# Where the squares of eight attention heads are added up: VectorE adds four tiles, TensorE sums one

## The chip, the cores and the metric

The kernel runs on one core of one Trainium2 chip. The core's engines each work through their own list of instructions in order and wait for one another on semaphores: TensorE (PE; its weight loads are PEld), VectorE (DVE), ScalarE (ACT), GpSimd (POOL) and SyncE (SP). The metric is the device time of one execution in microseconds, lower is better; a kernel's time is the median of its runs.

## The reference, cut to what matters

The program is a transformer block followed by a second, hybrid one, on 512 positions of width 1024. The change lies in the first block, between its attention and its output projection. Eight heads of windowed attention and four of differential attention give the 1024 columns of `mix`. The first 512 columns are normed together, each head of the other kind by itself:

```python
y_a = swa_sink_attention(...)                  # (B, 512, 8 * 64)
y_a = rms_norm(y_a, swa_out_g[layer])          # one mean of squares over all 512 columns
y_b = diff_attention(...)                      # 4 heads of 128 columns, each normed over its 128
mix = jnp.concatenate([y_a, y_b], axis=-1)
x = x + rms_norm(jnp.einsum("bse,ed->bsd", mix, w_out[layer]), attn_post_g[layer])

def rms_norm(x, g):
    xf = x.astype(jnp.float32)
    xf = xf * lax.rsqrt(jnp.mean(xf * xf, axis=-1, keepdims=True) + EPS)
    return (xf * g.astype(jnp.float32)).astype(x.dtype)
```

## The kernel before

Activations stand transposed: the 128 partitions hold columns of the model, the free dimension holds the 512 positions, so `MIX[:, c, :]` is a tile of 128 columns by 512 positions. Tiles 0 to 3 are the eight windowed heads, tiles 4 to 7 the four differential heads. A sum over columns is then a sum over partitions, and TensorE makes it: a product of a constant matrix (`O512`, filled with 1/512) with a tile of squares gives the mean in every partition. For tiles 0 to 3 four such products accumulate in one PSUM bank, `PX[:, 1, :]`. They are plain fp32, and each appears in the trace as two matmul records.

The attention stage is one loop over 32 units, `for w in range(32)`, written out by hand for every engine. Units 0 to 15 are four pairs of windowed heads by four blocks of queries, units 16 to 31 four differential heads by four blocks. The order on each engine is the order of the code; there is no scheduler. The steps that matter here, with their lines:

- TensorE, for each unit: the scores two units ahead (`diff_scores`, L475), the transposes of this unit's probabilities (`att_turn`, L491), every fourth unit the product with the values (`swa_pv` L504, `diff_pv` L528), then two pieces of an unrelated projection that fills the gaps (`fill_piece`, L424: six matmuls each, weights split in a high and a low part). Each weight panel of this filler has eight pieces; pieces 0 to 3 make one output tile and 4 to 7 the next in the same PSUM bank, so piece 4 waits until VectorE has copied the first tile away: `pe.wait_ge(once("fill1_out"), k + 1)`. For panel k = 4 that is the first filler piece of unit 18. After it stands, at the end of unit 18, `mix_sums(0)` (L517).
- VectorE, for each unit: on even units the copy of a filler tile (`fill1_out`, L1345 or L1348), the logits two units ahead (`att_logits`, L1317), the probabilities one unit ahead (`att_probs`, L1325 to L1334), and at units 5, 9, 13 and 17 the copy of a pair's output into `MIX` (`swa_out`, L1361). `mix_scale` (L1366) multiplies `MIX` by the factor that the mean gives.
- ScalarE, for each unit: the exponentials (`att_exp`, L862) and the copy of the transposes (`att_copy`, L876 and L878); at unit 17 the four squares (`mix_square(0)`, L891), which wait for the last `swa_out`; at unit 19 the factor (`factor("mix", ...)`, L809 to L813).
- ScalarE and GpSimd or VectorE split each weight panel (`hi`, L776; L317, L1195).

`link(ins)` on VectorE issues an instruction and waits for it before the next one.

Of the kernel before, what the change touches and what calls it, by code (L numbers as in the profile page):

```python
# [21 lines left out]
ALU = mybir.AluOpType  # L22
# [61 lines left out]
def build(nc, panels, xT, cols_in, lamv_in, wi_in, rgw_in, uk_in, uv_in, outT):  # L84
    spill = nc.dram_tensor("x2_spill", (P, DC, S), F32, kind="Internal").ap()
    with ExitStack() as ctx:
# [3 lines left out]
        def at(name, shape, kb, dt=F32):  # L90
            size = 4
            for n in shape[1:]:
                size *= n
            assert kb * KB + size <= 207.5 * KB, (name, kb, size)
            return nc.alloc_sbuf_tensor_at(name, shape, dt, offset=ARENA0 + int(kb * KB))

        def sem(name):
            return ctx.enter_context(nc.semaphore(name))
# [22 lines left out]
        MSQ = at("MSQ", [P, DC, S], 96)  # L121
# [55 lines left out]
        O512 = at("O512", [P, P], 203)  # L177
        O128 = at("O128", [P, P], 203.5)
# [5 lines left out]
        PX = ctx.enter_context(nc.psum_tensor("PX", [P, 4, S], F32))  # L184
# [53 lines left out]
        def once(name):  # L238

            if name not in named:  # L240
                named[name] = sem(name)
            return named[name]
# [80 lines left out]
        def _(pe):  # L323
# [107 lines left out]
            def out_pass(o, p, t, c, c0, xh_first=False):  # L431

                s = p % 2
                wh, wl = (w[:, s].rearrange("p a b -> p (a b)")[:, (c - c0) * S + t * P:(c - c0) * S + t * P + P] for w in (WH, WL))
                pe.matmul(o, wh, XH[:, c, :], start=(c == c0), stop=False)
                pe.matmul(o, wh, XL[:, c, :], start=False, stop=False)
                return pe.matmul(o, wl, XH[:, c, :], start=False, stop=(c == c0 + 3))
# [68 lines left out]
                mm.then_inc(once("swa_pv"), 1)  # L506

            def mix_sums(k):
                tiles = range(4) if k == 0 else [3 + k]
                if k == 0:  # L510
                    pe.wait_ge(consts, 9)
                    pe.wait_ge(once("v_copied"), 5)
                else:
                    pe.wait_ge(once("mix_r"), k)
                for c in tiles:
                    pe.wait_ge(once("mix_sq"), c + 1)
                    mm = pe.matmul(PX[:, 1, :], O512[:] if k == 0 else O128[:], MSQ[:, c, :], start=(c == tiles[0]),  # L517
                                   stop=(c == tiles[-1]))
                mm.then_inc(once("mix_sum"), 1)

            def diff_pv(h):
                pe.wait_ge(once("att_copied"), 16 + NB * h + NB)
# [35 lines left out]
            low_piece(14)  # L558
            low_piece(15)
            mix_sums(4)  # L560

            p = FIRST["out1"][0] + 2
            pe.wait_ge(w_lo, p + 1)
            pe.wait_ge(once("att_logits"), 64)
            for c in range(4, DC):
                pe.wait_ge(once("mix_split"), c + 1)
                for t in range(4):
                    mm = out_pass(PG[:, t, :], p, t, c, 4)
# [4 lines left out]
            for t in range(4):  # L573
# [8 lines left out]
                for c in range(4, DC):  # L582
                    mm = out_pass(o, p, t, c, 4)
                mm.then_inc(once("y1_tile") if t < 3 else panel_done, 1)
            for t in range(2):
                pe.wait_ge(sq, 4 + t)
                mm = pe.matmul(PX[:, 1, :], O1024[:], SQY[:, 6 + t, :], start=False, stop=(t == 1))
# [72 lines left out]
            for t in range(4):  # L660
# [3 lines left out]
                for m in range(2):  # L664
                    pe.matmul(PX[:, m, :], RGW[:, 0, 2 * t + m, :], XC[:, t % 2, m, :], start=True, stop=True)
                    mm = pe.matmul(PX[:, 2 + m, :], RGW[:, 1, 2 * t + m, :], XC[:, t % 2, m, :], start=True, stop=True)
# [493 lines left out]
        def _(dve):  # L1160
            step_ = Count(dve_step)

            def link(ins):

                step_(ins)
                dve.wait_ge(dve_step, step_.n)
# [136 lines left out]
            def att_logits(w):  # L1303
                qb, s = w % NB, w % 3
                dve.wait_ge(once("att_s"), w + 1)
                if w >= 3:
                    dve.wait_ge(once("att_turned"), w - 2)
                n = (qb + 1) * P if w >= 16 else P if qb == 0 else 256
                if w < 16:
                    j = w // NB  # L1310
                    dve.tensor_copy(PD[s][:, :, n:n + 1], NSK[:, 2 * j:2 * j + 2].rearrange("p (a b) -> p a b", b=1))
                for m in range(2):
                    if w < 16:
                        dist, first, slope = NDS[:, 256 - n:], NSK[:, 2 * j + m:2 * j + m + 1], SLOPES_1[PAIR_HEADS[j][m]]
                    else:
                        dist, first, slope = NECF[:, (3 - qb) * P:], 3e38, SLOPES_1[8 + w // NB - 4]
                    dve.tensor_tensor_reduce(out=PD[s][:, m, 0:n], in0=dist, in1=PG[:, 2 * (w % 2) + m, 0:n],  # L1317
                                             scale=-slope, scalar=first, op0=ALU.add, op1=ALU.min,
                                             accum_out=NM3[:, 2 * s + m:2 * s + m + 1]).then_inc(once("att_logits"), 1)

            def att_probs(w):
                qb, s = w % NB, w % 3
                den = DEN3[:, 2 * s:2 * s + 2]
                dve.wait_ge(once("att_exp"), w + 1)
                link(dve.reciprocal(den, den))  # L1325
                if w < 16:
                    n = P if qb == 0 else 256
                    for m in range(2):
                        ins = dve.tensor_scalar(PD[s][:, m, 0:n], PD[s][:, m, 0:n], den[:, m:m + 1], None, ALU.mult)
                else:  # L1330
                    n = (qb + 1) * P
                    link(dve.tensor_scalar(RTL, den[:, 1:2], LAM, None, ALU.mult))
                    link(dve.tensor_scalar(PD[s][:, 1, 0:n], PD[s][:, 1, 0:n], RTL, None, ALU.mult))
                    ins = dve.scalar_tensor_tensor(out=PD[s][:, 0, 0:n], in0=PD[s][:, 0, 0:n], scalar=den[:, 0:1],  # L1334
                                                   in1=PD[s][:, 1, 0:n], op0=ALU.mult, op1=ALU.subtract)
                ins.then_inc(once("att_probs"), 1)

            def fill1_out(k, m):
                tile = FILL_TILES[k][m]
                if m == 0:  # L1340
                    dve.wait_ge(once("fill1_half"), k + 1)
                else:
                    dve.wait_ge(panel_done, FIRST["fill1"][0] + k + 1)
                if 6 <= tile < 10:
                    ins = dve.scalar_tensor_tensor(out=PROJ[:, tile, :], in0=PX[:, 2, :], scalar=SCALE / SLOPES_1[2 + tile],  # L1345
                                                   in1=R[:], op0=ALU.mult, op1=ALU.mult)
                else:
                    ins = dve.tensor_tensor(PROJ[:, tile, :], PX[:, 2, :], R[:], ALU.mult)  # L1348
                ins.then_inc(evac if m else once("fill1_out"), 1)

            def low_out(t):
                if t % 4 == 3:
                    dve.wait_ge(panel_done, FIRST["out1"][0] + t // 4 + 1)
                else:
                    dve.wait_ge(once("low_tile"), t + 1 - t // 4)
                dve.tensor_copy(Y1[:, t, :] if t < 4 else PROJ[:, 10 + t, :], PX[:, 2, :])\
                    .then_inc(evac if t % 4 == 3 else once("low_out"), 1)

            def swa_out(j):
                dve.wait_ge(once("swa_pv"), j + 1)  # L1360
                dve.tensor_copy(MIX[:, j, :], PX[:, 3, :]).then_inc(once("swa_out"), 1)  # L1361

            def mix_scale(k):
                dve.wait_ge(once("mix_r"), k + 1)
                for c in range(4) if k == 0 else [3 + k]:
                    dve.scalar_tensor_tensor(out=MIX[:, c, :], in0=MIX[:, c, :],  # L1366
                                             scalar=col("swa_out", c) if k == 0 else SUBLN,
                                             in1=MR[:], op0=ALU.mult, op1=ALU.mult).then_inc(once("mix_y"), 1)
# [7 lines left out]
            def diff_out(h):  # L1376
                dve.wait_ge(once("diff_pv"), h + 1)
                dve.tensor_copy(MIX[:, 4 + h, :], PX[:, 3, :]).then_inc(once("diff_out"), 1)
# [5 lines left out]
            for w in range(32):  # L1384
                if 2 <= w <= 24 and w % 2 == 0:
                    fill1_out((w - 2) // 4, 0 if w % 4 == 2 else 1)
                if w >= 26:
                    low_out(w - 26)
                if w + 2 < 32:
                    att_logits(w + 2)  # L1390
                if w + 1 < 32:
                    att_probs(w + 1)
                if w % NB == 1 and w >= 5:
                    swa_out(w // NB - 1) if w <= 17 else diff_out(w // NB - 5)
                if w >= 20 and w % NB == 0:
                    mix_scale((w - 20) // NB)
                if w == 24:
                    mix_lo(0)
                if w >= 25 and w % NB == 1:
                    mix_lo((w - 21) // NB)  # L1400
# [276 lines left out]
            for qb in (1, 2, 3):  # L1677
                w = MD[:, OFF[qb]:OFF[qb] + (qb + 1) * P]
# [183 lines left out]
```

## Time and profile before

| | |
|---|---|
| median of 3 runs | 1415.3 us (1414.84 to 1415.87) |
| the profiled execution's own time | 1418.66 us |
| its span in the trace | 1416.4 us |
| PE busy in the span | 1338.6 us (95%) |
| DVE / ACT / POOL busy | 857.8 / 580.5 / 232.7 us (61% / 41% / 16%) |
| mean granted TensorE clock | 0.971 of 2.4 GHz |
| chain that ended last | PE 79%, DVE 14%, ACT 3% |

The profile is of one execution. Its span runs from the first to the last recorded instruction; 2.3 us of the execution's time lie around it. Times in the rows are microseconds from the start of the span unless they are marked ns. TensorE's clock has two levels, 1.2 and 2.4 GHz; a granted clock of 1.00 is the upper one all through a stretch, and 0.50 the lower one.

### The profile page before, as it was taken

The page shows a single profiled execution, that of the slowest core. Times are in us where ns is not written, and L with a number is a line of the kernel's source. Part 1 is how long each engine was busy: PE and PEld are TensorE (multiplying, and loading weights), DVE is VectorE, ACT ScalarE, POOL GpSimd, SP SyncE. Part 2 cuts the span into 40 slices and gives each one's busy share as a digit, 9 for nine tenths or more (in the row PEclk, how much of TensorE's full clock was granted, in tenths as well). Part 3 has the DMA queues.
Part 4 walks back from the last instruction along what each step waited for, and adds up shares of the span by engine and source line. Part 5 has one row for each costly group of instructions (what it writes and reads, how often), then busy time and mean ns, then how long its engine had stood idle before and what let it go on. Part 6 is the DMA issues. An engine that isn't in the chain of part 4 may idle for free.

```text
span 1416.4 us, 16189 instructions
## 1 busy us (share of the span) xinstructions
PE 1338.6 (95%) x6006; PEld 1040.6 (73%) x6006; DVE 857.8 (61%) x1471; ACT 580.5 (41%) x848; POOL 232.7 (16%) x181
## 2 busy tenths in 40 slices
PE   7899979899999999999999999999799989999996
PEld 6676557688888888888888767777568855667885
DVE  6345664678888368738853333569987256663242
ACT  5344545444434233323322344323555246554231
POOL 2322113000000000000000323420004511114451
PEclk9999989899999999999999999899899999999999
DMA  5211002022232223222322221402113210001411
GB/s 188 89 60 60 31 30 89 30 89 89 93 113 91 89 91 115 91 89 92 115 89 89 90 115 65 149 32 87 60 64 115 90 60 30 31 30 63 162 73 60
DMA packets 17785, 116.48 MB, mean 82 GB/s; under 512 B 1984, under 2 KB 2240, under 8 KB 4544
## 3 DMA queue, kind: packets, MB, share of 16 engines
q1 hardware_dynamic: 16320, 108.35, 21.6%
q10 hardware_dynamic: 1408, 7.37, 1.4%
q8 instruction: 36, 0.59, 0.2%
q14 instruction: 21, 0.17, 0.0%
HBM read 111.52 MB, written 4.19 MB: 82 GB/s over the span
## 4 chain that ended last, share of the span: by engine, by line
PE 79%; DVE 14%; ACT 3%; issue 2%; DMA 0%; POOL 0%; ACTq 0%; DVEq 0%; SPq 0%
PE PG L337 20%; PE PG L338 20%; PE PG L339 20%; PE PX L424 4%; PE PX L689 3%; PE PX L598 2%; PE PG L718 2%; PE PX L728 1%; DVE MD L1565 1%; DVE XC L1591 1%; DVE MD L1583 1%; DVE WL L1195 1%; ACT WH L776 1%; PE PX L373 1%; DVE SM L1580 1%
## 5 line engine op out<-in xcount | busy, mean ns | idle before, releaser
L317 POOL TENSOR_TENSOR WL<-RAW,WH 128x512 fp32r<-128x512 f32 x168 | 229.4, 1397 | 1151.1 <-ACT WH L776 1151.1
L337 PE MATMUL PG<-XH,WH 128*128 128x512 f32 x992 | 392.7, 396 | 16.2 <-DVE WL L1195 9.3
L338 PE MATMUL PG<-XL,WH 128*128 128x512 f32 x992 | 388.3, 391 | 0.0
L339 PE MATMUL PG<-XH,WL 128*128 128x512 f32 x992 | 388.2, 391 | 0.0
L776 ACT ACTIVATE WH<-RAW 128x2048 fp32r<-128x2048 f32 x100 | 191.4, 1914 | 384.7 <-PE PG L339 374.5
L337 PEld LDWEIGHTS PG<-XH,WH 128*128 128x128 f32 x992 | 187.5, 189 | 62.9 <-DVE WL L1195 11.9
L338 PEld LDWEIGHTS PG<-XL,WH 128*128 128x128 f32 x992 | 187.6, 189 | 39.7 <-issue 1.4
L339 PEld LDWEIGHTS PG<-XH,WL 128*128 128x128 f32 x992 | 187.5, 189 | 39.4
L1195 DVE TENSOR_TENSOR WL<-RAW,WH 128x2048 fp32r<-128x2048 f32 x58 | 132.7, 2287 | 18.8 <-ACT WH L776 18.7
L337 PE MATMUL PG<-AH,WH 128*128 128x512 f32 x256 | 99.6, 389 | 0.0
L338 PE MATMUL PG<-AL,WH 128*128 128x512 f32 x256 | 99.6, 389 | 0.0
L339 PE MATMUL PG<-AH,WL 128*128 128x512 f32 x256 | 99.6, 389 | 0.0
L959 ACT ACTIVATE Z<-Z 128x512 f32<-128x512 f32 x32 | 20.3, 633 | 164.7 <-DVE Z L1489 164.7
L1473 DVE TENSOR_TENSOR U<-PG,R 128x1024 f32<-128x1024 f32 x32 | 39.2, 1224 | 53.2 <-PE PG L339 48.5
L339 PEld LDWEIGHTS PG<-AH,WL 128*128 128x128 f32 x256 | 48.1, 188 | 10.0
L337 PEld LDWEIGHTS PG<-AH,WH 128*128 128x128 f32 x256 | 48.1, 188 | 10.0
L338 PEld LDWEIGHTS PG<-AL,WH 128*128 128x128 f32 x256 | 48.1, 188 | 9.9
L1508 DVE TENSOR_TENSOR FA<-PG,FA 128x1024 f32 (+1 forms) x12 | 14.7, 1224 | 64.6 <-PE PG L339 64.6
L337 PE MATMUL PG<-RH,WH 128*128 128x512 f32 x128 | 49.8, 389 | 0.0
L339 PE MATMUL PG<-RH,WL 128*128 128x512 f32 x128 | 49.8, 389 | 0.0
L947 ACT ACTIVATE C<-U,COL 128x512 f32<-128x512 f32 x64 | 48.2, 800 | 0.1
L1484 DVE SCALAR_TENSOR_TENSOR C<-U,COL,C 128x510 f32<-128x510 f32 x64 | 45.1, 747 | 3.8
(291 smaller groups left out, 1980.2 us busy)
## 6 DMA issues: line engine op xcount, KB each, us to landing
RAW<-panels SPq DMA_DIRECT2D x100, 1024.0 KB, 4.7
x_spill<-XT ACTq DMA_DIRECT2D x1, 2048.0 KB, 6.3
XT<-x_spill ACTq DMA_DIRECT2D x1, 2048.0 KB, 7.8
outT<-SQ SPq DMA_DIRECT2D x4, 512.0 KB, 3.0
XT<-xT ACTq DMA_DIRECT2D x2, 512.0 KB, 6.3
XT<-xT SPq DMA_DIRECT2D x2, 512.0 KB, 8.9
RGW<-rgw ACTq DMA_DIRECT2D x1, 1024.0 KB, 4.8
UK<-uk ACTq DMA_DIRECT2D x1, 512.0 KB, 5.7
```

The lines of the kernel that those rows point to most:

```text
L317: ins = pool.tensor_tensor(WL[:, s].rearrange("p a b -> p (a b)")[:, piece], RAW[:, s, piece], WH[:, s].rearrange("p a b -> p (a b)")[:, p ...
L337: pe.matmul(o, WH[:, s, c, ms], xh[:, c, :], start=(c == 0), stop=False)
L338: pe.matmul(o, WH[:, s, c, ms], xl[:, c, :], start=False, stop=False)
L339: mm = pe.matmul(o, WL[:, s, c, ms], xh[:, c, :], start=False, stop=(c == DC - 1))
L424: mm = pe.matmul(PX[:, 2, :], w[:, s, c, m * P:(m + 1) * P], x[:, c, :], start=(c == 0 and w is WH and x is XH), stop=(c == DC - 1 and w i ...
L598: mm = pe.transpose(PX[:, m, kb * P:(kb + 1) * P], src[u % 3][:, m, kb * P:(kb + 1) * P], IDN[:])
L689: mm = pe.matmul(PX[:, 2, :], w[:, s, c, m * P:(m + 1) * P], x[:, c, :], start=(c == 0 and w is WH and x is XH), stop=(c == DC - 1 and w i ...
L776: act.activation(WH[:, s].rearrange("p a b -> p (a b)"), RAW[:, s, :], ACT.Copy).then_inc(w_hi, 1)
L947: ins = act.activation(C[:, b, m, :], U[:, b, m, :], ACT.Identity, bias=col("cb", k + 32 * m), scale=col("cw2", k + 32 * m))
L1195: dve.tensor_tensor(WL[:, s].rearrange("p a b -> p (a b)"), RAW[:, s, :], WH[:, s].rearrange("p a b -> p (a b)").bitcast(F32), ALU.subtrac ...
L1473: dve.tensor_tensor(U[:, b], psum_of(p0 + b), rr(), ALU.mult).then_inc(evac, 1)
L1484: step_(dve.scalar_tensor_tensor(out=C[:, b, m, 2:], in0=U[:, b, m, 0:S - 2], scalar=col("cw0", n + 32 * m), in1=C[:, b, m, 2:], op0=ALU.m ...
```

## The change

The squares are still ScalarE's. VectorE now adds tiles 2 and 3 onto tiles 0 and 1 in one instruction of 1024 elements, then tile 1 onto tile 0 in one of 512, right after the last `swa_out` at unit 17. TensorE waits for that sum (`mix_acc`) and makes one product where it made four. The sums of the four later heads stay as they were.

```diff
             def mix_sums(k):
-                tiles = range(4) if k == 0 else [3 + k]
                 if k == 0:
                     pe.wait_ge(consts, 9)
                     pe.wait_ge(once("v_copied"), 5)
+                    pe.wait_ge(once("mix_acc"), 1)
                 else:
                     pe.wait_ge(once("mix_r"), k)
-                for c in tiles:
-                    pe.wait_ge(once("mix_sq"), c + 1)
-                    mm = pe.matmul(PX[:, 1, :], O512[:] if k == 0 else O128[:], MSQ[:, c, :], start=(c == tiles[0]),
-                                   stop=(c == tiles[-1]))
-                mm.then_inc(once("mix_sum"), 1)
+                    pe.wait_ge(once("mix_sq"), 4 + k)
+                pe.matmul(PX[:, 1, :], O512[:] if k == 0 else O128[:], MSQ[:, 0 if k == 0 else 3 + k, :], start=True, stop=True)\
+                    .then_inc(once("mix_sum"), 1)
...
                 if w % NB == 1 and w >= 5:
                     swa_out(w // NB - 1) if w <= 17 else diff_out(w // NB - 5)
+                if w == 17:
+                    dve.wait_ge(once("mix_sq"), 4)
+                    link(dve.tensor_tensor(MSQ[:, 0:2, :], MSQ[:, 0:2, :], MSQ[:, 2:4, :], ALU.add))
+                    dve.tensor_tensor(MSQ[:, 0, :], MSQ[:, 0, :], MSQ[:, 1, :], ALU.add).then_inc(once("mix_acc"), 1)
                 if w >= 20 and w % NB == 0:
                     mix_scale((w - 20) // NB)
```

Two lines fewer stand ahead of them, so VectorE's steps have line numbers that are smaller by two in the kernel after. In the order of its instructions VectorE has, at the end of unit 17 and the start of unit 18, before (the copy L1361 is `swa_out`, L1345 is `fill1_out` for the tile that filler piece 36 waits for; the brackets name the semaphores that are waited for):

```order
L1334 SCALAR_TENSOR_TENSOR PD_62<-PD_62,SM 128x384 [waits dve_step]
L1361 COPY MIX<-PX 128x512 [waits swa_pv]
L1345 SCALAR_TENSOR_TENSOR PROJ<-PX,R 128x512 [waits fill1_half]
L1317 ISA PD_64,SM<-NECF,PG 128x128 [waits att_turned,att_s]
L1317 ISA SM 128x1
```

and after:

```order
L1332 SCALAR_TENSOR_TENSOR PD_62<-PD_62,SM 128x384 [waits dve_step]
L1359 COPY MIX<-PX 128x512 [waits swa_pv]
L1395 TENSOR_TENSOR MSQ<-MSQ 128x1024 [waits mix_sq]
L1396 TENSOR_TENSOR MSQ<-MSQ 128x512 [waits dve_step]
L1343 SCALAR_TENSOR_TENSOR PROJ<-PX,R 128x512 [waits fill1_half]
L1315 ISA PD_64,SM<-NECF,PG 128x128 [waits att_turned,att_s]
L1315 ISA SM 128x1
```

The two additions, with the wait for the four squares, stand ahead of the copy of the filler tile and of all that follows it on VectorE.

TensorE at the end of unit 18 and the start of unit 19, before (L424 is the filler, L475 the scores of unit 21, L491 the transposes of unit 19):

```order
L424 MATMUL PX<-XH,WL 128x512
L517 MATMUL PX<-MSQ,O_123 128x512 [waits mix_sq,v_copied,consts]
L517 MATMUL PX<-MSQ,O_123 128x512 [waits mix_sq] x3
L475 MATMUL PG<-PROJ 128x256 [waits att_logits]
L475 MATMUL PG<-PROJ 128x256
L491 MATMUL PX<-IDN,PD_63 128x128 [waits att_copied,att_probs]
```

and after:

```order
L424 MATMUL PX<-XH,WL 128x512
L516 MATMUL PX<-MSQ,O_123 128x512 [waits mix_acc,v_copied,consts]
L475 MATMUL PG<-PROJ 128x256 [waits att_logits]
L475 MATMUL PG<-PROJ 128x256
L491 MATMUL PX<-IDN,PD_63 128x128 [waits att_copied,att_probs]
```

Three products are gone, and nothing else changes its place on TensorE; the twelve filler matmuls of unit 18, the first of which waits for `fill1_out`, still stand ahead of the product.

## Rows read from the trace of the kernel before

**Rows 1.** The profile's page: engines' busy time; chain that ended last, by engine.

```profile
PE 1338.6 (95%) x6006; PEld 1040.6 (73%) x6006; DVE 857.8 (61%) x1471; ACT 580.5 (41%) x848; POOL 232.7 (16%) x181
...
PE 79%; DVE 14%; ACT 3%; issue 2%; DMA 0%; POOL 0%; ACTq 0%; DVEq 0%; SPq 0%
```

**Rows 2.** The chain in order of time, 137 to 147: start us, us, what.

```profile
137.60 0.68 DVE MIX L1361
138.28 0.61 DVE PROJ L1345
...
138.93 3.02 PE PX L424 x12
141.95 3.43 PE PX L517 x8
145.39 0.63 PE PG L475 x4
146.02 0.60 PE PX L491 x4
...
146.64 0.60 ACT PTD L878
```

**Rows 3.** Timelines of ACT, DVE, PE: start us, us, engine, line, operation, tiles [idle].

```profile
138.31 2.19 ACT L891 ACTIVATE MSQ<-MIX 128x512 f32<-128x512 f32 x4 [3.42 <-DVE MIX L1361]
...
138.20 0.68 DVE L1345 SCALAR_TENSOR_TENSOR PROJ<-PX,R 128x512 f32<-128x512 f32 x1
...
138.93 0.50 PE L424 MATMUL PX<-XH,WH 128*128 128x512 f32 x1 [0.65 <-DVE PROJ L1345]
```

**Rows 4.** DVE's groups by line and shape: additions of two SBUF tiles | busy, mean ns.

```profile
L1172 DVE TENSOR_TENSOR SQY<-SQY 128x1024 f32<-128x1024 f32 x5 | 6.1, 1223 | 0.8 <-ACT SQY L817 0.7
...
L1435 DVE TENSOR_TENSOR XT<-XT,Y 128x512 f32<-128x512 f32 x8 | 5.5, 683 | 0.0
```

**Rows 5.** PE's timeline: the first matmul after four waits for another engine.

```profile
55.63 0.69 PE L488 MATMUL PX<-IDN,PD 128*128 128x128 f32 x2 [3.64 <-DVE PD L1329]
...
162.74 0.50 PE L424 MATMUL PX<-XH,WH 128*128 128x512 f32 x1 [0.65 <-DVE PROJ L1345]
...
212.87 0.50 PE L435 MATMUL PX<-XH,WH 128*128 128x512 f32 x1 [2.49 <-DVE PROJ L1356]
...
250.11 2.05 PE L579 MATMUL PX<-SQY,O 128*128 128x512 f32 x2 [3.27 <-DVE SQY L1172]
```

**Rows 6.** Stretches: busy of PE, PEld, DVE, ACT, POOL, then PE's clock, DMA.

```profile
58.00:61.00 3.00, 3.00 (x9) 2.13 (x7) 0.00 (x0) 0.00 (x0) 0.00 (x0) 0.50 0.61 254
61.00:65.00 4.00, 4.00 (x21) 2.87 (x20) 1.66 (x8) 1.58 (x5) 0.00 (x0) 0.94 0.00 0
...
163.00:167.00 4.00, 4.00 (x12) 3.15 (x12) 1.71 (x6) 2.31 (x9) 0.00 (x0) 0.61 0.47 199
...
190.00:194.00 4.00, 4.00 (x10) 3.13 (x11) 1.61 (x6) 1.00 (x5) 0.00 (x0) 0.50 0.00 0
...
212.00:217.00 5.00, 3.87 (x14) 2.55 (x14) 2.98 (x6) 3.07 (x6) 3.64 (x3) 1.00 0.00 0
...
255.00:260.00 5.00, 4.41 (x14) 2.71 (x13) 0.69 (x1) 1.55 (x2) 0.00 (x0) 0.90 0.00 0
```

**Rows 7.** The chain in order of time: two later filler pieces at the low clock.

```profile
162.74 4.54 PE PX L424 x12
...
189.72 0.80 PE PX L435
...
195.00 0.86 PE PX L517 x2
```

**Rows 8.** POOL's timeline around the change, and the four scalings of tiles 0 to 3.

```profile
132.14 5.12 POOL L317 TENSOR_TENSOR WL<-RAW,WH 128x512 fp32r<-128x512 f32 x4 [14.89 <-ACT WH L776]
154.21 6.40 POOL L317 TENSOR_TENSOR WL<-RAW,WH 128x512 fp32r<-128x512 f32 x4 [16.95 <-ACT WH L776]
...
L1366 DVE SCALAR_TENSOR_TENSOR MIX<-MIX,COL,MR x4: 747/1260/1774, 153.4 to 156.5; 128x512 f32<-128x512 f32 x4
```

## The prediction, made before the change was run

> **What bounds the kernel now.** I read the page first: TensorE is busy for 95% of the span and carries 79% of the chain that ended last, VectorE 14% [rows 1]. That says only that TensorE's time is worth something on average, so the next view is the chain in order of time at the changed place. There it runs: VectorE copies the last pair's output (`swa_out`, 137.60), then the filler tile (`fill1_out`, 138.28), TensorE starts the filler at 138.93, runs twelve matmuls in 3.02 us, the four sums in 3.43 us, the scores and transposes of units 21 and 19, and hands over to ScalarE at 146.64 [rows 2]. Two things are to be seen. The four products do stand on the path, so what is taken from them is a gain. And the filler piece ahead of them is held up by VectorE: TensorE sat idle for 0.65 us until the filler tile was copied [rows 3]. There is no slack on VectorE at just the spot where the change puts new work. The timeline of ScalarE is the third view: the four squares start at 138.31, when the last copy into `MIX` is done, and take 2.19 us [rows 3].
>
> **What is removed.** Eight matmul records of the sums take 3.43 us on the path [rows 2], so a product (two records) is 0.86 us. The later single products agree: 0.86 us for two records at 195.00 [rows 7]. Three products go: 3 x 0.86 = 2.58 us less on the path, at the full clock.
>
> **What is added.** VectorE, done with `swa_out` at 138.28, now waits for the fourth square: 138.31 + 2.19 = 140.50, plus some 0.05 us to see the semaphore, 140.55. The addition of 1024 elements takes 1.22 us (five like it, both inputs in SBUF) and is waited for by the next one, which takes 0.68 us (eight like it) [rows 4]. With 0.04 us for that hand-over VectorE is free at 140.55 + 1.22 + 0.04 + 0.68 = 142.49. Instructions in a row overlap by some 0.08 us there (the filler copy started at 138.20, before the 138.28 at which the copy ahead ended) [rows 2, 3], so `fill1_out` starts at 142.41.
>
> **What is queued behind it.** The filler copy `fill1_out` was to start at 138.20 and now starts at 142.41: 4.21 us late. TensorE waits for it with the twelve filler matmuls of unit 18, and nothing else stands before them that it could do, since the scores of unit 20 and the transposes of unit 18 come earlier in its order. So the filler starts at 138.93 + 4.21 = 143.14, and TensorE's idle stretch grows from 0.65 to 4.86 us. The wait for `mix_acc` itself costs nothing: the sum is there at 142.49, and the product comes only after the filler, at 146.16. Behind `fill1_out` on VectorE stand the logits of unit 20 and the probabilities of unit 19, 0.5 and 1.7 us of work; 4.2 us late they are done before 146, and TensorE needs the latter at 147.7, after the product and the scores. ScalarE's exponentials lie between and are short. None of these becomes the path.
>
> Path at the full clock: +4.21 - 2.58 = +1.63 us when the scores of unit 21 begin. From there ScalarE's copy at 146.64 and all that follows [rows 2] hang on TensorE's transposes, and I find no wait behind them that ends by something unshifted: the chain has no DMA in it (0% [rows 1]), and the weight panels are fetched when a buffer comes free, so they move along. The shift reaches the end.
>
> **The clock.** This is the term that the timelines of before don't hold, since there TensorE waited for only 0.65 us at this place. After an idle 3.64 us at 55.63 the granted clock was 0.50 in 58 to 61 and 0.94 in 61 to 65, which makes it low until about 61.5: 5.9 us of the lower level, half of it lost, 2.9 us. After 3.27 us of idle at 250.11 it was 0.90 in 255 to 260, low until 256.0: 5.9 us again, 2.9 us lost [rows 5, 6]. Before 162.74 the idle time was 1.56 us and 0.65 us close together; the granted clock in 163 to 167 was 0.61 and the twelve filler matmuls took 4.54 us where those at 138.93 took 3.02: 1.52 us lost [rows 2, 5 to 7]. An idle 2.49 us before 212.87 left it at 1.00 [rows 5, 6]. The idle stretch here would be 4.86 us, longer than the first two, so I expect the lower level (1.2 GHz). The price has 0 at one end (it falls and rises again all within the wait, or not at all) and 2.9 us at the other. TensorE is on the path for 5.1 us at the full clock after the wait (3.02 + 0.86 + 0.63 + 0.60), so there is enough for either price to bite. I take 2.2 us, halfway between the 1.5 and the 2.9 that rows show. The Trainium skill, "TensorE: Matmul & The Clock Gate", section "What's actually happening", has it that "the default state is throttled, and activity releases the throttle". By that rule a pause in TensorE's work costs more than its length, and the sum is not +1.6 but about +3.8; the rows with the 3.64 and the 3.27 us of idle agree, the one with 2.49 us does not show it.
>
> **A rule against the additions.** The four scalings of `MIX` tiles, each 128x512 with two inputs in SBUF, took 747 to 1774 ns, and the slow ones lie in the 6.40 us from 154.21 in which GpSimd was splitting a panel [rows 8]. The additions are of the same kind. Between 137.26 (132.14 + 5.12) and 154.21 GpSimd does nothing [rows 8], and they run from 140.5 to 142.5, so I price them undisturbed. Were they to meet a panel, each could be longer by up to the 1.03 us between the fastest and the slowest scaling, 2 us in all. The Trainium skill, "SBUF — State Buffer", section "SBUF: two separate sides", says that a VectorE instruction with two SBUF inputs and a GpSimd one that reads SBUF take a shared port pair in turns, each for its whole length. By that rule alone the sum would be as much as 2 us worse; here the trace has the two apart.
>
> **Sum.** +4.21 - 2.58 + 2.2 = +3.8 us. Made against the profiled execution that is 1418.66 + 3.8 = 1422.5 us; that execution lies 3.4 us above the median of the runs, of which nothing belongs to the change. Against the median: 1415.3 + 3.8 = 1419.1 us.
>
> **Rivals.**
> - *No clock price.* The wait grows as worked out, but the clock stays up, or falls and rises within the wait. For it: 2.49 us at 212.87 cost nothing. Against it: 4.86 us is twice that, and both waits over 3 us are followed by the low level. Time: +1.6, 1416.9 us.
> - *Not slower: the later low stretches go.* A shift of the work changes where the later pauses fall, and with them whether the clock drops. At 162.74 the low clock cost 1.52 us, and from 189.72 to 195.00 twelve filler matmuls took 5.28 us instead of some 2.8 to 3.0, another 2.3 [rows 2, 7]. If both went, the sum would be 3.8 - 1.5 - 2.3 = 0.0, or -2.2 with no price at the new wait: 1413.1 to 1415.3 us. It decides as soon as the later pauses give back more than 3.8 us. Against it: these pauses are waits for VectorE that the change leaves in place, such as the 2.49 us at 212.87, and nothing shortens them.
> - *More than worked out.* The clock stays low on through unit 19 and into the pauses of the next units, as it is low all through 190 to 194 in the trace of before [rows 6]: 2 to 3 us more than my price, 1421.5 us.
> - *The change does less than it says*, that is TensorE gains little because the four products overlapped with something: against it, the eight records are back to back on the path. Its price would be at most the 2.58 us, giving 1421.7 us; I put it with the case before.
>
> **How the numbers follow.** A measurement of this kernel can tell 0.2%, 2.8 us, from no change; the bound for slower is 1418.1 us. The forecast (+2.4 to +5.2, as the clock price goes from 0.8 to 3.6) has 0.66, and nine tenths of that lie over the bound. No clock price has 0.20, all within 0.2%. Not slower has 0.07, of which some 0.04 is faster by over 0.2%. More than worked out has 0.07. Slower is 0.59 + 0.07 = 0.66, same 0.30, faster 0.04. The range takes in the case without a clock price with half a microsecond of room below and the one with a longer low stretch above: 1416.0 to 1421.5 us.
>
> **What would show it.** In the profile after: VectorE idle for about 2.2 us before the addition of 1024, until ScalarE's squares; additions of 1.22 and 0.68 us; TensorE idle for 4.9 us before the filler of unit 18, with VectorE's filler copy as the releaser; a single product of 0.86 us (1.7 at the low clock); a granted clock below 1.00 in the 4 us after the wait, and the twelve filler matmuls there over 4 us long; ScalarE's copy L876 (L878 before) 3.8 us later than at 146.64, and the same distance up to the end of the attention stage. The forecast is wrong if TensorE's idle stretch is much under 4 us (then something hid VectorE's wait), if the clock stays at 1.00 there, or if the distance at the end of the stage isn't that at unit 19 (then the later pauses decide).

## The result: 0.3% slower, as forecast

| | median, us | runs | range, us |
|---|---|---|---|
| before | 1415.76 | 7 | 1414.84 to 1416.42 |
| changed | 1420.49 | 7 | 1417.88 to 1421.93 |

The ratio is 1.0030, with a 95% interval of 1.0019 to 1.0041: +4.2 us, between +2.7 and +5.8. This ratio, like every ratio with an interval below, is estimated from all runs and is not the quotient of the two medians, which lie 4.7 us apart. The forecast was +3.8 us, 1419.1 us. The same kernel was measured again later beside 16 runs of the one before: 1.0018 (1.0009 to 1.0027), +2.6 us. Both intervals exclude no change, and both hold the forecast's ratio of 1.0027 or touch it.

### The profile page after: what moved, and what is told of

It is laid out like the page before. It is cut to its first block, busy times and chain, and to the rows that moved or that the text cites. A ratio compares the mean times of both kernels' runs of the same rounds, so it can differ in the third digit from the quotient of the medians.

```text
span 1418.6 us, 16179 instructions
## 1 busy us (share of the span) xinstructions
PE 1336.6 (94%) x6000; PEld 1039.9 (73%) x6000; DVE 859.7 (61%) x1473; ACT 580.6 (41%) x848; POOL 232.7 (16%) x181
## 4 chain that ended last, share of the span: by engine, by line
PE 79%; DVE 14%; ACT 4%; issue 2%; DMA 0%; POOL 0%; ACTq 0%; DVEq 0%; SPq 0%
PE PG L337 20%; PE PG L339 20%; PE PG L338 20%; PE PX L424 4%; PE PX L687 3%; PE PX L596 2%; PE PG L716 2%; PE PX L726 1%; DVE MD L1567 1%; DVE XC L1593 1%; DVE MD L1585 1%; DVE WL L1193 1%; ACT WH L774 1%; PE PX L373 1%; DVE SM L1582 1%
```

## The profile after

In the page of the changed kernel the engines' shares hardly move; TensorE is busy for 2.0 us less and the span is 2.2 us longer.

```profile
span 1418.6 us, 16179 instructions
...
PE 1336.6 (94%) x6000; PEld 1039.9 (73%) x6000; DVE 859.7 (61%) x1473; ACT 580.6 (41%) x848; POOL 232.7 (16%) x181
```

That is all a page can tell: an engine with less to do, in a longer execution. The chain in order of time (start us, us, what), at the place of [rows 2]:

```profile
136.90 0.61 DVE MIX L1359
137.51 0.02 issue
137.54 2.20 ACT MSQ L889 x4
139.73 0.02 issue
139.76 1.24 DVE MSQ L1395
141.00 0.02 issue
141.02 0.04 DVE MSQ L1396
141.06 0.57 issue
141.63 0.69 DVE PROJ L1343
142.32 0.04 issue
142.37 4.54 PE PX L424 x12
146.91 0.86 PE PX L516 x2
147.77 0.63 PE PG L475 x4
148.40 0.60 PE PX L491 x4
...
149.02 0.60 ACT PTD L876
```

Four squares on ScalarE and two additions on VectorE now stand on the path ahead of the filler tile's copy; before, the copy followed `swa_out` at once. (The chain splits the second addition's 0.69 us into 0.04 and 0.57 us of "issue", because the copy behind it waits for nothing but its turn on VectorE.) The product is down from 3.43 to 0.86 us, and the twelve filler matmuls between them are up from 3.02 to 4.54 us. VectorE's and TensorE's timelines name the waits (in brackets: idle before, and what ended it):

```profile
139.76 1.23 DVE L1395 TENSOR_TENSOR MSQ<-MSQ 128x1024 f32<-128x1024 f32 x1 [2.25 <-ACT MSQ L889]
141.02 0.69 DVE L1396 TENSOR_TENSOR MSQ<-MSQ 128x512 f32<-128x512 f32 x1
...
142.37 0.79 PE L424 MATMUL PX<-XH,WH 128*128 128x512 f32 x1 [4.86 <-DVE PROJ L1343]
```

The stretches show the clock (the number after POOL's):

```profile
137.00:142.00 5.00, 0.51 (x3) 0.27 (x3) 2.71 (x4) 3.97 (x9) 0.00 (x0) 0.68 0.59 210
142.00:146.00 4.00, 3.63 (x9) 2.90 (x10) 2.26 (x9) 0.88 (x4) 0.00 (x0) 0.55 0.00 0
146.00:150.00 4.00, 4.00 (x20) 2.52 (x20) 1.45 (x8) 0.96 (x2) 0.00 (x0) 1.00 0.00 0
```

It fell to the lower level inside the idle stretch, at about 138.8 (0.68 over five microseconds is 3.2 us at the lower level), and came back at 145.6 (0.55 over four microseconds is 3.6 us), 3.2 us after the filler had begun.

**A measure for this place.** Whole executions of one kernel differ by up to 6 us here (before: 1412.55 to 1418.71 us in 35 runs), so the experiments are judged by two numbers: the ratio over many runs, and a distance inside the trace, from the start of the squares on ScalarE to the start of its copy of unit 19. Before: 146.64 - 138.31 = 8.33 us [rows 2, 3]. Changed: 149.02 - 137.54 = 11.48 us, that is +3.15. This distance is free of what happened earlier in the execution and of later pauses. Counted from the start of the span the copy came only 2.38 us later (149.02 against 146.64), because this execution was already 0.77 us ahead when the squares began (137.54 against 138.31); that is why the page shows a span only 2.2 us longer.

## The experiments

### The additions moved behind the filler copy

```diff
-                if w == 17:
+                if w == 18:      # now behind fill1_out and att_logits(20), ahead of att_probs(19)
                     dve.wait_ge(once("mix_sq"), 4)
                     link(dve.tensor_tensor(MSQ[:, 0:2, :], MSQ[:, 0:2, :], MSQ[:, 2:4, :], ALU.add))
                     dve.tensor_tensor(MSQ[:, 0, :], MSQ[:, 0, :], MSQ[:, 1, :], ALU.add).then_inc(once("mix_acc"), 1)
```

> The changed kernel, with VectorE's wait for the squares and its two additions moved from the end of unit 17 to unit 18, behind the filler copy and the logits of unit 20. Theory (the loss is the filler copy queued behind the additions, plus the low clock that TensorE's 4.86 us of idle time bring): the filler starts 0.65 us after the transposes again, the additions run from about 0.9 us after the filler began and are done some 0.5 us after the filler ends, the probabilities of unit 19 are then what TensorE waits for; the path at ScalarE's copy of unit 19 is 1.7 us shorter than before, the clock stays at 1.00 there: 1.0 to 2.0 us faster than before, 1414 us. Rival A (the additions cost VectorE time wherever they stand, 1.9 us, because VectorE is the path): as slow as the changed kernel less the clock, +1.6 us. Rival B (the one product is no gain, since the four overlapped with something): no faster than before.

Measured: 1412.79 us against 1416.27, ratio 0.9975 (0.9967 to 0.9984). The instructions are those of the changed kernel, with VectorE's wait and its two additions behind the filler copy and the logits in place of ahead of them, and the result has the other sign. VectorE's and TensorE's timelines:

```profile
136.31 0.68 DVE L1343 SCALAR_TENSOR_TENSOR PROJ<-PX,R 128x512 f32<-128x512 f32 x1
...
138.64 1.23 DVE L1391 TENSOR_TENSOR MSQ<-MSQ 128x1024 f32<-128x1024 f32 x1 [1.25 <-ACT MSQ L889]
139.91 0.69 DVE L1392 TENSOR_TENSOR MSQ<-MSQ 128x512 f32<-128x512 f32 x1
...
137.04 0.50 PE L424 MATMUL PX<-XH,WH 128*128 128x512 f32 x1 [0.65 <-DVE PROJ L1343]
...
140.74 1.10 PE L516 MATMUL PX<-MSQ,O 128*128 128x512 f32 x2 [0.69 <-DVE MSQ L1392]
```

VectorE still waits for the squares (1.25 us), but while TensorE works on the filler. The filler starts 0.65 us idle, as before; the product now waits 0.69 us for the additions. The distance is 143.10 - 136.42 = 6.68 us, or -1.65, where the theory had -1.7. Two details of the expectation were off: the additions began 1.6 us after the filler and not 0.9, and what TensorE waited for was the additions, not the probabilities of unit 19. So rival A, by which the additions cost the same wherever they stand, is out, and so is rival B. The additions still cost 0.93 us of the 2.58 here, since the product waits for them, but no longer the 4.21 us that they cost ahead of the copy.

### The wait alone

```diff
                     swa_out(w // NB - 1) if w <= 17 else diff_out(w // NB - 5)
+                if w == 17:
+                    dve.wait_ge(once("mix_sq"), 4)
```

> The kernel before with one line added: at the end of unit 17 VectorE waits for the four squares, and adds nothing; TensorE still makes four products. Theory (the wait ahead of the filler copy is paid in full, and a long idle stretch of TensorE costs the clock on top): the filler copy starts 2.35 us later, TensorE is idle for 3.0 us in place of 0.65, the clock falls to the lower level for the filler: +2.35 + 1.5 = +3.9 us, at the least +2.35. Rival (the wait is hidden by slack on VectorE, the additions alone cost): 0 to +0.5 us.

Measured: 1419.64 us against 1416.27, ratio 1.0016 (1.0004 to 1.0027). One line that moves no data costs. The chain (start us, us, what):

```profile
138.52 2.20 ACT MSQ L891 x4
140.72 0.02 issue
140.74 0.70 DVE PROJ L1345
141.44 0.04 issue
141.49 5.49 PE PX L424 x12
146.97 3.54 PE PX L517 x8
150.51 0.63 PE PG L475 x4
151.14 0.60 PE PX L491 x4
...
151.76 0.60 ACT PTD L878
```

TensorE was idle for 3.00 us, the filler took 5.49 us against 3.02, and the distance is 151.76 - 138.52 = 13.24 us: +4.91. Of that 2.35 us is the wait, as expected, and 2.6 us the clock (2.47 in the filler, 0.11 in the products), 1.1 us more than I had set down. The clock was low from about 140.2 (0.78 in 138 to 142), before the filler began, until about 147.1:

```profile
142.00:147.00 5.00, 5.00 (x13) 3.86 (x12) 1.62 (x4) 1.26 (x7) 0.00 (x0) 0.50 0.00 0
147.00:152.00 5.00, 5.00 (x18) 2.42 (x18) 0.81 (x5) 0.23 (x1) 0.00 (x0) 0.99 0.00 0
```

The additions are not needed to explain a loss, and the rival's 0 to +0.5 us is out by the trace and by the ratio's interval (+0.6 to +3.8 us).

### One product and nothing else

```diff
-                tiles = range(4) if k == 0 else [3 + k]
+                tiles = [3] if k == 0 else [3 + k]
                 if k == 0:
                     pe.wait_ge(consts, 9)
                     pe.wait_ge(once("v_copied"), 5)
...
                 for c in tiles:
                     pe.wait_ge(once("mix_sq"), c + 1)
```

> The kernel before with TensorE's four products cut to the one of tile 3 alone and no additions, so the mean of squares leaves out tiles 0 to 2; it still waits for all four squares. Theory (three products of 0.86 us stand on the path): -2.6 us, with the clock as before at this place. Rival (the products overlap with other work): -0.5 us or less.

This kernel leaves three quarters of the columns out of the mean; it serves to time the path and nothing else.

Measured: 1412.84 us against 1416.27, ratio 0.9975 (0.9965 to 0.9985). The distance is 142.36 - 136.25 = 6.11 us, or -2.22, where 2.58 were taken out. TensorE's timeline says where most of the missing 0.36 us went:

```profile
139.72 1.02 PE L517 MATMUL PX<-MSQ,O 128*128 128x512 f32 x2
141.67 0.66 PE L491 MATMUL PX<-IDN,PD 128*128 128x128 f32 x4 [0.29 <-DVE PD L1334]
```

The transposes of unit 19 now wait 0.29 us for VectorE's probabilities, and those, by the chain, for ScalarE's exponentials, which are queued behind the four squares. With the products gone, what is late next is the squares themselves.

### TensorE kept busy in the wait

```diff
+                if w == 18:
+                    pe.wait_ge(once("v_copied"), 5)
+                    for _ in range(20):
+                        pe.matmul(PX[:, 1, 0:P], O1024[:], O1024[:], start=True, stop=True)
                 if w < 24:
                     fill_piece(2 * w)
```

> The changed kernel, with twenty 128x128 products of constants, whose result nobody reads, on TensorE ahead of the filler of unit 18, where it stood idle for 4.86 us. Theory (1.5 us or more of the loss is the clock that falls in that idle stretch): the filler starts at the same time after VectorE's copy, the granted clock stays at 1.00, the twelve filler matmuls take 2.8 to 3.0 us in place of 4.54, and the kernel is 1.5 to 3 us faster than the changed one, that is +1.6 us against before. Rival (the clock isn't what makes the filler slow, or the loss lies elsewhere): same time as the changed kernel, +4 us.

Measured: 1417.81 us against 1416.27, ratio 1.0004 (0.9993 to 1.0015). TensorE's timeline (two records for each of the twenty products), its chain, and the stretches with their clock:

```profile
137.05 4.63 PE L550 MATMUL PX<-O 128*128 128x128 f32 x40
142.07 0.50 PE L424 MATMUL PX<-XH,WH 128*128 128x512 f32 x1 [0.39 <-DVE PROJ L1347]
```

```profile
142.07 3.01 PE PX L424 x12
145.09 0.86 PE PX L516 x2
```

```profile
137.00:142.00 5.00, 4.68 (x42) 4.49 (x40) 2.71 (x5) 3.97 (x9) 0.00 (x0) 1.00 0.59 210
142.00:146.00 4.00, 3.93 (x16) 2.68 (x18) 1.96 (x9) 0.88 (x4) 0.00 (x0) 1.00 0.00 0
```

The filler starts as late as in the changed kernel, but the clock stays up and it takes 3.01 us. The distance is 147.20 - 137.24 = 9.96 us: +1.63, which is the sum at the full clock to the hundredth. The clock is thus shown to be a term of its own: 1.52 us in the first trace of the changed kernel. That rests on the trace: the interval of the ratio (-1.0 to +2.1 us) holds +1.63 and no change alike, and excludes only the rival's +4.

### The changed kernel again

> The changed kernel once more, unedited, with more runs. Theory (the change itself makes 1.6 us, the low clock behind the wait 1.5 to 2.6, as in two traces so far): +3.2 to +4.2 us against before, and in the trace a step of that size at the filler of unit 18, with less than 1 us more from there to the end of the attention stage. Rival (later pauses add to it in each execution): a further step of over 1 us in the trace behind unit 20, and +5 us.

Measured: 1419.51 us against 1417.54, ratio 1.0018 (1.0009 to 1.0027). The distance is 150.02 - 138.37 = 11.65 us: +3.32. The distance lies inside the expected +3.2 to +4.2 us, the ratio's +2.6 below it. The idle time ahead of the filler is 4.85 us long; the filler takes 4.71 us. Up to the end of the attention stage no further loss came behind it, on the contrary. Where the filler of the next head took 4.54 us before [rows 7] and 4.61 us in the first trace of the changed kernel, it took 3.02 us here, behind the same two idle stretches of 1.57 and 0.65 us:

```profile
166.12 3.02 PE PX L424 x12
```

and where the two sums at 250 us ran at the lower level before [rows 5], with 2.05 us for the first, here the same wait of 3.27 us was followed by the upper one (timeline, then the stretch with its clock):

```profile
251.12 1.10 PE L577 MATMUL PX<-SQY,O 128*128 128x512 f32 x2 [3.27 <-DVE SQY L1170]
```

```profile
249.00:254.00 5.00, 2.88 (x9) 1.78 (x10) 1.94 (x2) 0.25 (x1) 0.00 (x0) 1.00 0.01 2
```

From before 250 to behind it this execution gains some 2.8 us on the first one; near 1190 us, where the first trace had the upper level throughout, it loses 1.6 us again. It is the same code: such a step belongs to the execution, not to the change. The filler of the next head shows the same spread over the other kernels: behind idle stretches that are equal to 0.02 us it took 3.02 us in the traces of the additions moved back and of TensorE kept busy, and 5.49 us in that of one product and nothing else.

### More traces of the kernels before and after

> The kernel before, unedited, for a second trace of it. Theory (where the clock is low in the later pauses is chance and not the change): against the first trace of before, the path is within 0.1 us at unit 18 (filler to ScalarE's copy of unit 19) and differs by over 1 us at one or more of the pauses at 55, 163, 190 or 250 us. Rival (those places are fixed for a kernel and move by the change alone): no step over 0.5 us anywhere against the first trace.

> The kernel before, unedited, for a third trace. Expectations as for the second: no step at unit 18, and steps of over 1 us at some of the later pauses if these are chance, none if they are the kernel's.

> The changed kernel, unedited, for a third trace of it. Theory (the new wait brings the low clock every time, at a price that hangs on when the clock falls and rises): a step of +2.7 to +4.7 us at unit 18 against a trace of before, TensorE idle for 4.86 us there, and the filler behind it 4.3 to 5.6 us long. Rival (the two traces so far were chance): a step of 1.6 us.

These executions took 1417.51, 1416.27 and 1418.40 us. For the kernel before, ScalarE's copy comes as far behind the last `swa_out` as in the first trace, to 0.02 us. But the pauses at 55, 163, 190 and 250 us also fell out alike in all three traces of it, within 0.25 us each. What differs is some 0.6 us ahead of 38 us and, in the third, 1.5 us near 1222 us. So the expectation of over 1 us at one of the four named pauses was a miss both times; only the third trace has a step of that size, at a later one. Three traces of before hardly show the spread, while the traces of the changed kernel do. In the third of these TensorE's idle stretch falls at the same place, the filler takes 4.34 us and the distance is 147.74 - 136.46 = 11.28 us: +2.95, near the lower end of what was expected.

### Squares and additions spread over the units

The squares of tiles 0, 1 and 2 are taken at units 6, 10 and 14, tiles 1 and 2 are added on at units 11 and 15, and only tile 3 is left for units 17 and 18.

```diff
+                if w in (6, 10, 14):                                   # ScalarE
+                    act.wait_ge(once("swa_out"), w // NB)
+                    act.activation(MSQ[:, w // NB - 1, :], MIX[:, w // NB - 1, :], ACT.Square).then_inc(once("mix_sq"), 1)
...
+                if w == 18:                                            # VectorE, behind att_logits(20)
+                    dve.wait_ge(once("mix_sq"), 4)
+                    dve.tensor_tensor(MSQ[:, 0, :], MSQ[:, 0, :], MSQ[:, 3, :], ALU.add).then_inc(once("mix_acc"), 1)
...
+                if w in (11, 15):
+                    dve.wait_ge(once("mix_sq"), w // NB)
+                    link(dve.tensor_tensor(MSQ[:, 0, :], MSQ[:, 0, :], MSQ[:, w // NB - 1, :], ALU.add))
```

> One product, as in the changed kernel, but with the work spread out: ScalarE squares tiles 0, 1 and 2 at units 6, 10 and 14, soon after each is there, VectorE adds tile 1 and tile 2 onto tile 0 at units 11 and 15, and only tile 3 is squared at unit 17 and added behind the filler copy and the logits of unit 20. Theory (the path there is TensorE's filler and product; the sum of squares is now done before the filler ends): the transposes of unit 19 wait for nothing, 2.5 us shorter at ScalarE's copy of unit 19 than before, -2.6 us or a little less, 1413.5 us; 0.8 us faster than the kernel with the two additions behind the logits. Rival (the early squares and additions push back TensorE's transposes at units 7, 11 and 15, where ScalarE or VectorE are on the path): they cost 0.5 to 2 us there and the total is no better than with the two additions behind the logits.

> The kernel with the squares and additions spread over the units, unedited, for a second trace. Theory: a step of -2.6 us at unit 18, none over 0.3 us between units 5 and 16. Rival (the early squares push back TensorE in some executions): a step of over 0.3 us there.

Measured: 1412.79 us against 1417.54, ratio 0.9970 (0.9958 to 0.9982); its second traced execution took 1414.72 us. It is faster than both kernels. The chain:

```profile
137.35 0.68 DVE MIX L1362
138.03 0.61 DVE PROJ L1346
138.64 0.04 issue
138.68 3.02 PE PX L424 x12
141.70 0.86 PE PX L516 x2
142.56 0.63 PE PG L475 x4
143.19 0.60 PE PX L491 x4
...
143.81 0.60 ACT PTD L876
```

This is [rows 2] with 0.86 in the place of 3.43 and nothing else changed. From `swa_out` to ScalarE's copy it is 143.81 - 137.35 = 6.46 us, where it was 146.64 - 137.60 = 9.04: -2.58, all of the three products, and the second trace gives the same. Neither trace shows a step of the path at units 5 to 16. Against the version with both additions behind the logits the path is 0.9 us shorter; their medians are equal (1412.79), but the two were measured at different times, beside medians of before of 1416.27 and 1417.54, and the intervals of their ratios overlap. So that 0.9 us is shown by the traces alone.

The last column is what follows behind the place of the change: the span of the trace less the start of ScalarE's copy of unit 19.

| kernel | distance against before, us | by terms | ratio (95%) | from there to the end, us |
|---|---|---|---|---|
| before, three traces | 0 | | | 1269.8, 1269.4, 1268.2 |
| changed, three traces | +3.15, +3.32, +2.95 | +4.21 - 2.58 + clock 1.5, 1.7, 1.3 | 1.0030 (1.0019 to 1.0041), 1.0018 (1.0009 to 1.0027) | 1269.6, 1265.7, 1268.4 |
| changed, TensorE kept busy | +1.63 | +4.21 - 2.58 | 1.0004 (0.9993 to 1.0015) | 1266.6 |
| wait alone | +4.91 | +2.35 + clock 2.6 | 1.0016 (1.0004 to 1.0027) | 1267.5 |
| one product alone | -2.22 | -2.58 + 0.36 | 0.9975 (0.9965 to 0.9985) | 1270.4 |
| additions later | -1.65 | -2.58 + 0.93 | 0.9975 (0.9967 to 0.9984) | 1266.7 |
| spread over the units, two traces | -2.58 | -2.58 | 0.9970 (0.9958 to 0.9982) | 1267.8, 1270.3 |

## Why the prediction was right

- **Three products on the path, -2.58 us.** Right in size: 3.43 us became 0.86, and the kernel with the spread squares gets all of it. That rules out the rival in which they overlapped with something.
- **The filler copy 4.21 us late.** Right to the hundredth: TensorE's idle stretch was to be 4.86 us and was 4.86 us in the trace, with VectorE's filler copy as its end. The wait for the squares was 2.25 us, the additions took 1.23 and 0.69 us, and GpSimd was idle beside them, as forecast; what the additions would have cost beside a panel, no run here shows.
- **+1.63 us at the full clock.** Shown by keeping TensorE busy: +1.63.
- **The clock.** That the wait brings the low clock was right, and the size high: I took 2.2 us, halfway between 1.5 and 2.9, and the three traces have 1.5, 1.7 and 1.3. The midpoint had no mechanism behind it. A shorter idle stretch, 3.00 us in the one trace with the wait alone, cost 2.6 us, so the price doesn't grow with the length of the wait. What it follows in these four traces is how much of the low stretch was left when the filler began, the rest having passed while TensorE was idle anyway. By the granted clock that was 3.2 us (until 145.6), 3.7 us (0.52 in 143 to 147, so until 146.8) and 2.9 us (0.98 in 144 to 148, so until 144.2) in the changed kernel, and 5.6 us with the wait alone. Half of each, the time lost at half the clock, is 1.6, 1.8, 1.4 and 2.8 us; measured were 1.5, 1.7, 1.3 and 2.6. The rival "no clock price" fell, and so did "more than worked out": the clock was at 1.00 from 146 to 150.
- **A row that is not shown.** The 1.56 us of idle time that the prediction counts ahead of 162.74 stand in none of its rows; the trace of before has them, but the clock fell only after them: it was still 1.00 in 163.0 to 163.5, and low in all but 0.9 us of the 163 to 167 at 0.61. So that row is no example of a clock that falls inside a wait.

```profile
161.54 0.55 PE L491 MATMUL PX<-IDN,PD 128*128 128x128 f32 x3 [1.56 <-DVE PD L1334]
```

- **No other engine takes over.** Right for the changed kernel; but with less ahead of them the exponentials behind the squares would (0.29 us, in the kernel with one product).
- **The shift reaches the end.** In the first trace the path is 3.15 us longer at unit 18 and no step of over 0.1 us follows until the end. The third, beside the third trace of before, keeps the shift as well (1268.4 and 1268.2 us from there to the end). In the second, two pauses give back 1.6 and 2.8 us, more than the change had cost: its span is 1415.7 us, under the 1416.4 of the first trace of before. The prediction argued against this rival that the later pauses are left in place. They were, but the clock behind them was not the same. The rival "not slower" is thus what single executions can look like, but the ratios over many runs exclude it as the usual case.

The forecast of +3.8 us lies 0.5 to 0.9 us above all three traces, by the clock term; that it comes within 0.4 us of the first ratio's +4.2 is luck.

What stays open: the first ratio stands for +4.2 us and the second for +2.6, around the 3.1 us of the three traces; both intervals hold 3.1. In the four kernels that shorten the path or keep TensorE busy the gain over many runs is some 1 to 2 us larger than the distance tells (-3.5 for -1.65, -3.5 for -2.22, -4.3 for -2.58, +0.6 for +1.63), and the wait alone costs less than its distance (+2.3 for +4.91). The last column of the table shows where it can come from: behind the place of the change the traces of the edited kernels take 1265.7 to 1270.4 us, those of before 1268.2 to 1269.8, and the kernel with the spread squares has both 1267.8 and 1270.3. Whether that is later pauses falling out differently by chance, or more often one way when the path ahead is shorter, one or two traces of each can't tell.

## What to carry to other kernels

Work put on an idle-looking engine is priced by what is queued behind it, not by its own length: look in the timeline for the instruction that follows at that place and who waits for it. Here the same two additions lost 3 us of path ahead of a copy and gained 1.7 behind it. When the wait reaches TensorE, add a term for its clock: a range read from pauses of the same trace, not a point, since the same pause fell out either way here. And spread the new work out early, so that only the last partial sum is late: then the whole gain of the shorter product is had.

## What the runs showed of the chip that I had not expected

The price of the low clock did not follow the length of the pause: 2.6 us after 3.00 us of idle time, 1.3 to 1.7 us after 4.86 us. It followed what was left of the low stretch when TensorE's work began again. And the same pause in the same code (3.27 us at 250 us; 1.57 and 0.65 us close together ahead of the next head's filler) was followed by the lower level in one execution and by the upper one in another, which alone moves an execution by 2.8 and 1.6 us: as much as most of what was measured here, and a reason to read the size of such a change from a distance inside the trace.
